# Expert blocks filled by gathers of the tokens' rows, through a table of token numbers by slot, in place of a scatter of those rows

## Chip, cores and metric

One core of one Trainium2 chip runs the whole program. The metric is device time in microseconds (us) of one launch; the median of several runs is given. Everything is fp32.

## The reference, cut to what matters

Two layers over 384 tokens of width 1024: 128 context tokens and 256 latent tokens. Layer 0 mixes by gated linear attention and RWKV-7 scans, layer 1 by latent and differential attention. After the mixer, each layer has a top-2 mixture of 16 experts:

```
scores = sigmoid(t @ w_router); sel = scores + b_router
best group of 4 experts (sum of its two highest sel); top 2 experts in it
gates = scores of the two, divided by their sum
hidden = silu(t @ w_gate[e]) * (t @ w_up[e])      # 1024 -> 512
out    = sum over the two experts of gate * (hidden @ w_down[e])   # 512 -> 1024
```

A layer's experts have 16 x 3 weight matrices of 2 MB, about 100 MB in all, which come from memory once. Each token is computed by its two experts alone.

## The kernel before

**Stages.** Layer 0's mixer, its experts (about 560 to 885 us of the profile), layer 1's mixer, its experts (about 1195 to the end). The order of the work is written out by hand for each engine: every engine has its own program, and waits on semaphores. `when(name)` is the moment at which an engine told an event by name; `steps_of(L, step, i, c)` is a step of expert block c.

**Routing.** TensorE (`router`, `scores`) makes the scores; it also transposes the normalised tokens into rows, which ScalarE copies to `htok` (three tiles of 128 tokens). VectorE (`route`, L2344 on) finds each token's two experts, its place within each expert by products with ones that TensorE makes, ranks the experts by their load, and gives each (token, expert) pair a row. It tells "dst" when the 6 x 128 row numbers `rows_i` are there, and "rows" when the experts' numbers by block are in `xtab`, from which SyncE (SP) reads which expert's weights to load.

**Blocks.** The 16 experts are computed as blocks, c = 0 to 15. Ranks 2 to 7 have room for 96 rows (CAP), the others for 64 (SMALL). Blocks 0, 1 and so on alternate between two buffers. Blocks 0 and 1 (experts 0 and 2) are picked straight from `htok` by products with ones and zeros (`rows_pick`). The rows of the other blocks travel through memory: GpSimd (POOL) issues six indirect DMAs (L639) that scatter the 768 rows of `htok` to a tensor `dispatched`, waits until all have landed (L641), and then reads block by block back (L646, L648, L651), each when the buffer is free, which is when the block two before has been transposed.

**One block on TensorE:** transpose its rows (`rows_T`, or `rows_pick`), gate and up (`gate_up`), transpose the hidden rows (`hidden_T`), down (`down`). The program's order is: pick 0, gate_up 0, pick 1, hidden_T 0, gate_up 1, rows_T 2, down 0, hidden_T 1, gate_up 2, rows_T 3, down 1, and so on in pairs. ScalarE and VectorE copy and combine between those; ScalarE stores the outputs of a block to `expert_out`. At the end POOL gathers each token's two output rows from there (L655), and VectorE adds them with their gates.

**Weights.** SP loads the 48 matrices of a layer, in the order gate, up and down of each block interleaved as they are needed, into six places of 2 MB. The first six go before the router is done. Load 7 (up of block 2) and load 8 (down of block 1) stand behind the wait for "rows", as all later ones. Each load waits for its place: a gate's place is free when the gate product of the block two before is done, and so on. All loads of SP share one queue, and so the weights arrive in order.

**Zeros.** In the early mixer, ScalarE writes zeros over the whole of `dispatched` (8.3 MB) and over the last part of `expert_out` (3.4 MB).

Experts with more tokens than room have extra blocks, behind a test that all engines make (`n_extra`); in the profiled execution there were none.

Of the kernel before, what the change touches and what calls it, by code (L numbers as in the profile page):

```python
# [22 lines left out]
P = 128  # L23
# [36 lines left out]
for _n, _w in [("earlier", 128), ("ones", 128), ("tri16", 256), ("pos", 16), ("rank", 16), ("key", 16), ("extra", 144), ("slots", CAP)]:  # L60
    _M[_n] = (_at, _w)
    _at += _w
# [8 lines left out]
FULL0, SMALL0 = LEAD * SMALL, LEAD * SMALL + FULL * CAP  # L71
XROW = FULL * CAP + (NE - FULL) * SMALL
# [32 lines left out]
def build(nc, io, known):  # L105
# [3 lines left out]
    with ExitStack() as ctx:  # L109
# [56 lines left out]
        Xd = nc.dram_tensor("dispatched", (ROWS, D), F32, kind="Internal").ap()  # L166
        Yd = nc.dram_tensor("expert_out", (ROWS, D), F32, kind="Internal").ap()
        arena_words = 27272
# [130 lines left out]
        htok = take(TILES * D).rearrange("p (t d) -> p t d", t=TILES)  # L299
        hot = take(2 * TILES * CAP).rearrange("p (e t n) -> p e t n", e=2, t=TILES)  # L300
# [104 lines left out]
        def _(sp):  # L405
# [15 lines left out]
            def early(l, m, e, place):  # L421
                weights(l, m, e, place, w_place[place])
# [16 lines left out]
            def experts(l):  # L439
# [24 lines left out]
                sp.wait_ge(*when("rows", l))  # L464
                e3, e4 = expert(slice(3, 4)), expert(slice(4, 5))
# [3 lines left out]
                early(l, 2, LEADERS[1], 1)  # L469
                gate_w(L, l, None, 3, 1, e3)  # L470
# [17 lines left out]
                with sp.If(n_extra > 0):  # L488
# [3 lines left out]
                    with sp.Fori(0, NX) as i:  # L492
# [4 lines left out]
                        sp.wait_ge(*steps_of(X, "xT_p", i, -1))  # L497
                        sp.dma_start(xb[0:CAP, 0, :], Xd[bass.ds(i * CAP + XROW, CAP), :]).then_inc(X["rows"][0][0], 16)
# [27 lines left out]
        def _(pool):  # L526
# [103 lines left out]
            def experts(l):  # L630
# [55 lines left out]
        def _(pe):  # L686
# [852 lines left out]
        def _(act):  # L1539
# [33 lines left out]
            def gate_rows(l, s):  # L1573
                if l == 0 and s == 0:
                    act.wait_ge(sem("xd_zero"), 32)
# [257 lines left out]
            def experts(l):  # L1833
# [5 lines left out]
                silu(L, None, 1, 1, SMALL)  # L1839
                for c in range(LEAD):  # L1840
                    rows_copy(L, None, c + 2, c)
                    store(L, None, c, c, slice(c * SMALL, (c + 1) * SMALL), SMALL)
                    silu(L, None, c + 2, c, cap_of(c + 2))
                with act.Fori(1, half - 2) as i:
                    rows_copy(L, i, 2, 0)
                    store(L, i, 0, 0, bass.ds(i * CAP + (FULL0 - CAP), CAP), CAP)
# [1101 lines left out]
```

## Time and profile before

| | |
|---|---|
| median of 3 runs | 1517.27 us (1516.02 to 1518.22) |
| profiled execution, its own time | 1523.06 us |
| its span, first to last instruction | 1521.3 us |
| mean granted TensorE clock | 0.926 |
| TensorE matmuls busy | 1308.7 us (86%) |
| VectorE, ScalarE, GpSimd busy | 522.0, 337.8, 164.7 us |
| DMA | 355.18 MB, mean 233 GB/s |
| scatters of rows | 12 (6 a layer) |
| expert weight loads | 96 of 2048 KB, 24.5 us in the median from issue to landing |

Each engine's busy time is a mean over stages with different limits, and so it doesn't say what sets the end of one. The rows further down are read by stage: the chain of waits says what released what, the windows give the engines' busy time, the granted clock and the share of the DMA engines in a stretch, and the timelines give single instructions. A DMA's landing time runs from its issue to its last semaphore update. A DMA share of 1.0 means that all 16 engines move data all the time.

### The profile page before, as it was taken

Reading aid. Unit: us, or ns where it says so; the run is one execution under the profiler, and the core shown is the slowest. Engines: PE = TensorE matmul, PEld = TensorE weight load, DVE = VectorE, ACT = ScalarE, POOL = GpSimd, SP = SyncE. Lnnn points to the kernel's source line nnn. Section 1 sums busy time; section 2 is a strip of 40 time slices with the busy share of each in tenths; the row PEclk is TensorE's granted clock in tenths of the full one; section 3 lists DMA queues with packets and bytes.
Section 4 is the critical chain, followed back from the end, with each engine's and each line's share of the span. In section 5 each row is a group of like instructions: output and inputs, shape, how many; then the busy total and the mean of one; then the engine's idle time right before and its main releaser. Section 6 shows DMA issues by size and latency. Waiting matters only on the chain.

```text
span 1521.3 us, 38803 instructions
## 1 busy us (share of the span) xinstructions
PE 1308.7 (86%) x16856; PEld 911.4 (60%) x16856; DVE 522.0 (34%) x1148; ACT 337.8 (22%) x671; POOL 164.7 (11%) x238
## 2 busy tenths in 40 slices
PE   5989999989998987699898669877899859998882
PEld 2448844468887455478776334455574637877651
DVE  1324444145556734011111053457544521111103
ACT  2223221143223131000000043333541300000001
POOL 2003310024333001000000030010000010000001
PEclk8999999999999989799999969988979888999997
DMA  9841159831001175799999882234304478999995
GB/s 396 300 156 59 59 201 315 301 145 59 29 33 59 56 287 214 279 382 379 397 403 417 358 305 76 91 112 181 135 32 166 177 306 304 377 396 395 386 422 194
DMA packets 42230, 355.18 MB, mean 233 GB/s; under 512 B 5707, under 2 KB 10651, under 8 KB 23792
## 3 DMA queue, kind: packets, MB, share of 16 engines
q1 hardware_dynamic: 21456, 302.11, 50.3%
q0 software_dynamic: 8832, 29.07, 5.7%
q10 hardware_dynamic: 11808, 22.03, 4.4%
q8 instruction: 107, 1.75, 0.5%
q14 instruction: 27, 0.22, 0.0%
HBM read 322.17 MB, written 31.01 MB: 232 GB/s over the span
## 4 chain that ended last, share of the span: by engine, by line
PE 65%; DMA 18%; DVE 7%; issue 7%; ACT 3%; POOL 1%; SPq 0%; ACTq 0%; POOLq 0%; DVEq 0%
PE PB L695 59%; DMA arena<-in_w_moe 11%; PE PB L698 6%; DVE arena L2019 3%; DMA dispatched<-arena,rows_i 3%; ACT arena L1546 1%; DMA ring<-in_w_mod 1%; DMA expert_out<-arena 1%; DMA arena<-expert_out,rows_i 1%; DVE small L2032 1%; POOL dispatched L639 1%; DVE arena L2026 1%; DMA arena<-dispatched 1%; DVE x L2019 0%; DVE arena L2023 0%
## 5 line engine op out<-in xcount | busy, mean ns | idle before, releaser
L695 PE MATMUL PB<-arena 64*64 64x64 f32 (+8 forms) x9500 | 478.5, 297 | 45.8 <-DMA arena<-in_w_moe 31.2
L695 PEld LDWEIGHTS PB<-arena 64*64 64x64 f32 (+3 forms) x9500 | 374.4, 131 | 144.9 <-issue 77.1
L695 PE MATMUL PB<-ring,hT 128*128 128x512 f32 (+1 forms) x720 | 314.0, 592 | 7.2 <-DVE hT L2022 3.6
L695 PEld LDWEIGHTS PB<-ring,hT 128*128 128x128 f32 x720 | 137.4, 194 | 167.4 <-issue 162.7
L695 PE MATMUL PB<-ring,arena 128*32 128x256 f32 (+2 forms) x3712 | 209.3, 380 | 9.8 <-DMA ring<-in_w_moe 6.9
L695 PEld LDWEIGHTS PB<-ring,arena 128*32 128x32 f32 x3712 | 171.4, 110 | 39.1 <-issue 9.7
L698 PE MATMUL PB<-cst,arena 128*128 128x128 f32 (+2 forms) x758 | 117.1, 296 | 83.7 <-DMA arena<-dispatched 40.5
L1546 ACT ACTIVATE arena<-PB 128x256 f32<-128x256 f32 (+3 forms) x217 | 106.4, 490 | 330.2 <-PE PB L695 279.1
L698 PEld LDWEIGHTS PB<-cst,arena 128*128 128x128 f32 (+2 forms) x758 | 90.0, 155 | 128.4 <-issue 43.4
L2442 DVE TENSOR_TENSOR arena<-arena,PB 128x256 f32<-128x256 f32 (+1 forms) x32 | 15.1, 471 | 284.6 <-PE PB L695 165.8
L550 POOL TENSOR_TENSOR arena<-arena,cst 128x256 f32<-128x256 f32 x72 | 49.2, 699 | 264.9 <-DVE arena L2019 245.2
L695 PE MATMUL PB<-ring,scT 128*32 128x512 f32 x384 | 57.6, 716 | 22.2 <-DMA ring<-in_w_mod 16.2
L2019 DVE TENSOR_TENSOR arena<-arena,PB 128x256 f32<-128x256 f32 (+1 forms) x116 | 51.0, 440 | 72.0 <-PE PB L695 68.0
L2019 DVE TENSOR_TENSOR arena<-arena 128x512 f32<-128x512 f32 (+7 forms) x120 | 68.1, 567 | 10.5 <-ACT arena L1546 6.4
L1807 ACT ACTIVATE arena<-PB 128x384 f32<-128x384 f32 x32 | 15.7, 491 | 235.7 <-PE PB L698 209.1
L2029 DVE COPY arena<-PB 128x512 f32<-128x512 f32 (+5 forms) x60 | 30.9, 515 | 102.2 <-PE PB L695 94.0
L2453 DVE COPY arena<-PB 128x256 f32<-128x256 f32 (+1 forms) x32 | 15.2, 474 | 131.9 <-PE PB L695 131.9
L1820 ACT ACTIVATE arena<-PB 128x256 f32<-128x256 f32 (+1 forms) x32 | 13.6, 424 | 144.2 <-PE PB L695 144.2
L1813 ACT ACTIVATE arena<-PB 128x256 f32<-128x256 f32 (+1 forms) x32 | 13.5, 423 | 141.4 <-PE PB L695 141.4
L1546 ACT ACT_TABLE_LOAD x27 | 34.6, 1283 | 37.2 <-DVE small L2022 19.6
L1546 ACT ACTIVATE gate<-PB 128x512 f32<-128x512 f32 x40 | 23.9, 597 | 67.8 <-PE PB L695 67.4
L695 PE MATMUL PB<-arena,cst 128*128 128x512 f32 (+1 forms) x80 | 35.8, 642 | 2.7 <-ACT arena L1546 2.7
(150 smaller groups left out, 905.2 us busy)
## 6 DMA issues: line engine op xcount, KB each, us to landing
arena<-in_w_moe SPq DMA_DIRECT2D x50, 2048.0 KB, 24.5
ring<-in_w_moe SPq DMA_DIRECT2D x46, 2048.0 KB, 24.6
ring<-in_w_mod SPq DMA_DIRECT2D x24, 2048.0 KB, 8.3
ring<-in_w_mix SPq DMA_DIRECT2D x22, 2048.0 KB, 8.7
dispatched<-gate ACTq DMA_DIRECT2D x1, 8320.0 KB, 51.4
arena<-dispatched POOLq DMA_DIRECT2D x12, 384.0 KB, 10.9
arena<-dispatched POOLq DMA_DIRECT2D x16, 256.0 KB, 9.3
expert_out<-gate ACTq DMA_DIRECT2D x1, 3456.0 KB, 22.2
```

What stands on the lines that cost most here:

```text
L550: nc.gpsimd.tensor_tensor(out, a, b, ALU.mult).then_inc(*tick("pool", *name))
L639: pool.indirect_dma_start(Xd, bass.IndirectOffsetOnAxis(ap=rows_i[:, 3 * ch + t:3 * ch + t + 1], axis=0), htok[:, t, :], None).then_inc(se ...
L695: return nc.tensor.matmul(out, lhsT, rhs, start=start, stop=stop, **k)
L698: return nc.tensor.transpose(out, in_, ident[0:n, 0:n])
L1546: step(nc.scalar.activation(out, in_, f, **k), *name)
L1807: nc.scalar.activation(xT[:, b, 0:4 * CAP], PB[:, 0, 0:4 * CAP], ACT.Copy).then_inc(L["S"]["xT_a"], 1)
L2019: step(V.tensor_tensor(out, a, b, op), *name)
L2026: step(V.scalar_tensor_tensor(out=out, in0=a, scalar=s, in1=b, op0=op0, op1=op1), *name)
L2029: step(V.tensor_copy(out, a), *name)
L2032: step(V.tensor_reduce(out, a, AX.X, op), *name)
L2442: V.tensor_tensor(hid[:, b, 0:n], sil[:, b, 0:n], PB[:, 4 + b, 0:n], ALU.mult).then_inc(L["S"]["hid"], 1)
L2453: V.tensor_copy(yb[:, b, n:2 * n], PB[:, 7, 0:n]).then_inc(L["S"]["y_v"], 1)
```

## The change

Empty slots and rows are laid out anew. Every block, by rank, has 96 rows in `expert_out`, though it still uses 64 or 96 of them; so a slot's number is 96 times its block's rank plus its place. From the slot of each (token, expert) pair VectorE makes two arrays of ones and zeros: `at_row` (which of 96 places) and `at_block` (which of 25 blocks, times the token's number). Six small products on TensorE (`table`) sum them to a table of 96 by 25 token numbers, which VectorE copies as integers to `tab`; an empty slot has token 0. TensorE makes the table at the head of block 1's pick; VectorE's copy stands behind "rows".

ScalarE stores `htok`, tile by tile, to a tensor `tokens` in memory as soon as each tile is copied (three DMAs of 512 KB). POOL waits for those and for the table, and then issues one indirect DMA a block that gathers its rows (96 or 64) from `tokens` into the block's buffer. The scatters, the wait for them, the tensor `dispatched` and its zeros are gone; in their place zeros go over rows 64 to 95 of each of the 16 blocks in `expert_out` (2 MB). POOL's loop over blocks is written out, and it tests for extra blocks itself; their rows were loaded by SP before.

On SP, the wait for "rows" and the two reads of expert numbers move behind loads 7 and 8, which need no number that is computed.

The diff, with only constants, renamed semaphores and the store's row arithmetic left out:

```diff
+RANK = [0, 1, 2, 8, 3, 9, 4, 10, 5, 11, 6, 12, 7, 13, 14, 15]
+XROW = NE * CAP
...
+        tab = ctx.enter_context(nc.sbuf_tensor("tab", [P, 32], I32))
+        Hd = nc.dram_tensor("tokens", (NTOK, D), F32, kind="Internal").ap()
...
-                sp.wait_ge(*when("rows", l))
-                e3, e4 = expert(slice(3, 4)), expert(slice(4, 5))
                 sp.wait_ge(*steps_of(L, "ga", None, 0))
                 early(l, 1, LEADERS[2], 0)
                 sp.wait_ge(*steps_of(L, "gu", None, 0))
                 early(l, 2, LEADERS[1], 1)
+                sp.wait_ge(*when("rows", l))
+                e3, e4 = expert(slice(3, 4)), expert(slice(4, 5))
...
-                pool.wait_ge(sem("xd_zero"), 32)
-                pool.wait_ge(*when("dst", l))
-                for t in range(TILES):
-                    pool.wait_ge(*when("htok", l, t))
-                    for ch in range(2):
-                        pool.indirect_dma_start(
-                            Xd, bass.IndirectOffsetOnAxis(ap=rows_i[:, 3 * ch + t:3 * ch + t + 1], axis=0),
-                            htok[:, t, :], None).then_inc(sem("dispatched"), 16)
-                pool.wait_ge(sem("dispatched"), 96 * (l + 1))
                 L = base_loop[l]
-                with pool.Fori(1, half - 1) as i:
-                    pool.wait_ge(*steps_of(L, "xT_p", i, -2))
-                    pool.dma_start(xb[0:CAP, 0, :], Xd[bass.ds(i * CAP + (FULL0 - CAP), CAP), :]).then_inc(x_land[0], 16)
-                    pool.wait_ge(*steps_of(L, "xT_p", i, -1))
-                    pool.dma_start(xb[0:SMALL, 1, :], Xd[bass.ds(i * SMALL + (SMALL0 - SMALL), SMALL), :]).then_inc(x_land[1], 16)
-                for b in range(2):
-                    pool.wait_ge(*steps_of(L, "xT_p", None, NE - 4 + b))
-                    pool.dma_start(xb[0:SMALL, b, :], Xd[XROW - (2 - b) * SMALL:XROW - (1 - b) * SMALL, :]).then_inc(x_land[b], 16)
+
+                def gather(b, cap, col, landed):
+
+                    pool.indirect_dma_start(xb[0:cap, b, :], None, Hd,
+                                            bass.IndirectOffsetOnAxis(ap=tab[0:cap, col:col + 1], axis=0)).then_inc(landed, 16)
+
+                pool.wait_ge(sem("h_stored"), 48 * (l + 1))
+                pool.wait_ge(*when("table", l))
+                for c in range(2, NE):
+                    if c >= 4:
+                        pool.wait_ge(*steps_of(L, "xT_p", None, c - 2))
+                    gather(c % 2, cap_of(c), RANK[c], x_land[c % 2])
+                n_extra = nc.gpsimd.value_load(xtab[0:1, 31:32], min_val=0, max_val=NX)
+                with pool.If(n_extra > 0):
+                    X = extra_loop[l]
+                    pool.wait_ge(*steps_of(L, "xT_p", None, NE - 2))
+                    for i in range(NX):
+                        pool.wait_ge(*steps_of(X, "xT_p", None, i - 1))
+                        gather(0, CAP, NE + i, X["rows"][0][0])
...
+            def table(l):
+
+                pe.wait_ge(*when("blocks", l))
+                claim(3, "table", l)
+                for j in range(6):
+                    ins = mm(PB[0:CAP, 3, 0:NE + NX], at_row[:, j, :], at_block[:, j, :], j == 0, j == 5)
+                ins.then_inc(*tick("pe", "table_p", l))
+
             def rows_pick(L, l, c):
 
                 pe.wait_ge(*when("hot", l, c))
+                if c == 1:
+                    table(l)
...
-                        act.dma_start(Xd.rearrange("(b p) d -> p b d", p=80), bc(zeros[0:80, :], 1, ROWS // 80))\
-                            .then_inc(sem("xd_zero"), 16)
+                        act.dma_start(Yd[0:XROW, :].rearrange("(b p) d -> p b d", p=CAP)[SMALL:CAP, :, :], bc(zeros[SMALL:CAP, :], 1, NE))\
+                            .then_inc(sem("y_zero"), 16)
...
+                    act.wait_ge(*when("htok", l, t))
+                    act.dma_start(Hd[t * P:(t + 1) * P, :], htok[:, t, :]).then_inc(sem("h_stored"), 16)
...
-                ts(base, rk, float(LEAD + FULL), float(LEAD), ALU.min, ALU.max)
-                ts(base, base, float(CAP - SMALL), float(LEAD * (CAP - SMALL)), ALU.mult, ALU.subtract)
-                stt(base, rk, float(SMALL), base, ALU.mult, ALU.add)
+                ts(base, rk, float(CAP), None, ALU.mult, None)
...
-                    red(rec[:, 0:3], v16(f))
-                    cp(rows_i[:, 3 * ch:3 * ch + 3], rec[:, 0:3], *(("dst", l) if ch else ()))
+                    red(picked[:, 3 * ch:3 * ch + 3], v16(f))
+
+                nb = NE + NX
+                ge6 = c2[:, 0:6 * (nb + 1)].rearrange("p (j b) -> p j b", j=6)
+                tt(ge6, bc(picked, 2, nb + 1), bc(M("edge"), 1, 6), ALU.is_ge)
+                red(block, ge6[:, :, 1:nb + 1])
+                tt(at_block, ge6[:, :, 0:nb], ge6[:, :, 1:nb + 1], ALU.subtract)
+                tt(at_block, at_block, bc(M("token"), 2, nb), ALU.mult)
+                stt(place_in, block, -float(CAP), picked, ALU.mult, ALU.add)
+                tt(at_row, bc(place_in, 2, CAP), bc(M("low"), 1, 6), ALU.is_equal, "blocks", l)
+                cp(rows_i[:, :], picked, "dst", l)
...
+                dve.wait_ge(*when("table_p", l))
+                cp(tab[0:CAP, 0:nb], PB[0:CAP, 3, 0:nb], "table", l)
```

## Rows read from the trace of the kernel before

**Rows 1.** Chain of waits, layer 0's entry: start us, us, what
```profile
593.19 24.34 DMA dispatched<-arena,rows_i
618.42 4.13 DMA arena<-dispatched
```

**Rows 2.** Windows: us, engines' busy us (instructions), PEclk, DMA share, GB/s
```profile
570.00:585.00 15.00, 13.32 (x146) 11.17 (x150) 11.94 (x49) 4.27 (x8) 0.00 (x0) 1.00 0.01 2
610.00:620.00 10.00, 0.00 (x0) 0.00 (x0) 0.00 (x0) 0.00 (x0) 1.12 (x2) 0.50 0.69 286
620.00:632.00 12.00, 9.40 (x110) 6.01 (x114) 1.31 (x3) 0.88 (x2) 0.53 (x1) 0.66 0.42 107
632.00:712.00 80.00, 80.00 (x1382) 63.89 (x1375) 10.39 (x21) 7.21 (x16) 2.57 (x5) 1.00 1.01 386
712.00:855.00 143.00, 123.91 (x2018) 95.88 (x2020) 16.33 (x35) 11.20 (x25) 3.08 (x6) 0.96 1.01 405
```

**Rows 3.** Timeline of SP's queue, both layers: start us, us, line, operation, tiles, count
```profile
590.66 0.33 SPq L419 DMA_DIRECT2D ring<-in_w_moe  x1
...
598.53 0.34 SPq L419 DMA_DIRECT2D ring<-in_w_moe  x1
...
629.81 0.34 SPq L419 DMA_DIRECT2D arena<-in_w_moe  x1
...
1234.50 0.34 SPq L419 DMA_DIRECT2D ring<-in_w_moe  x1
1237.80 27.21 SPq L419 DMA_DIRECT2D arena<-in_w_moe  x2
```

**Rows 4.** Timeline of VectorE, end of the routing of layer 0
```profile
585.72 0.17 DVE L2029 CAST rows_i<-arena 128x3 int32<-128x3 f32 x1
585.92 0.31 DVE L2019 TENSOR_TENSOR arena<-arena 128x144 f32<-128x144 f32 x1
...
588.58 0.17 DVE L2029 CAST xtab<-arena 128x16 int32<-128x16 f32 x1
```

**Rows 5.** Timeline of TensorE, layer 0; in brackets idle us before it, and releaser
```profile
570.36 2.18 PE L695 MATMUL PB<-small,arena 128*128 128x16 f32 x18 [0.54 <-DVE small L2019]
...
588.05 5.43 PEld L695 LDWEIGHTS PB<-arena 128*128 128x128 f32 x48 [0.41 <-DVE arena L2019]
...
598.13 3.64 PE L695 MATMUL PB<-arena 128*32 128x256 f32 x64
...
622.60 1.54 PE L698 MATMUL PB<-cst,arena 96*128 96x96 f32 x8 [20.82 <-DMA arena<-dispatched]
```

**Rows 6.** Timeline of POOL: a scatter of layer 0, a gather at its end
```profile
586.76 1.04 POOL L639 DMA_INDIRECT dispatched<-arena,rows_i  x1 [32.02 <-DVE arena L2032]
...
874.21 0.94 POOL L655 DMA_INDIRECT arena<-expert_out,rows_i  x1 [0.30 <-issue]
```

**Rows 7.** DMA issues of 871:885, 712:855, 499:500, 629.5:630, 1264.5:1265: KB each, us to landing
```profile
arena<-expert_out,rows_i POOLq DMA_INDIRECT x6, 5.7
...
arena<-dispatched POOLq DMA_DIRECT2D x2, 384.0 KB, 11.0
...
ring<-in_w_moe SPq DMA_DIRECT2D x1, 2048.0 KB, 7.7
...
arena<-in_w_moe SPq DMA_DIRECT2D x1, 2048.0 KB, 8.9
...
arena<-in_w_moe SPq DMA_DIRECT2D x1, 2048.0 KB, 9.4
```

**Rows 8.** DMA queues of 712:855, then 871:885: packets, MB, share of engines
```profile
q0 software_dynamic: 544, 1.84, 4.0%
...
q0 software_dynamic: 864, 3.15, 63.5%
```

**Rows 9.** The zero fill's issue, and the chain of waits beside it
```profile
dispatched<-gate ACTq DMA_DIRECT2D x1, 8320.0 KB, 51.4
...
233.60 70.22 PE PB L695 x196
```

More of the change, by code:

```diff
@@ L59 @@
 CAP = SETS * GRP
-for _n, _w in [("earlier", 128), ("ones", 128), ("tri16", 256), ("pos", 16), ("rank", 16), ("key", 16), ("extra", 144), ("slots", CAP)]:
+for _n, _w in [("earlier", 128), ("ones", 128), ("tri16", 256), ("pos", 16), ("rank", 16), ("key", 16), ("extra", 144), ("slots", CAP),
+               ("edge", NE + 10), ("low", CAP), ("token", 6)]:
     _M[_n] = (_at, _w)
@@ L299, in build @@
         htok = take(TILES * D).rearrange("p (t d) -> p t d", t=TILES)
+        at_row = take(6 * CAP).rearrange("p (j n) -> p j n", j=6)
+        at_block = take(6 * (NE + NX)).rearrange("p (j n) -> p j n", j=6)
         hot = take(2 * TILES * CAP).rearrange("p (e t n) -> p e t n", e=2, t=TILES)
@@ L1574, in gate_rows @@
                 if l == 0 and s == 0:
-                    act.wait_ge(sem("xd_zero"), 32)
+                    act.wait_ge(sem("y_zero"), 32)
                 for n in range(4):
@@ L1839, in experts, with rows_of @@
                 silu(L, None, 1, 1, SMALL)
+                def rows_of(c):
+                    return slice(CAP * RANK[c], CAP * RANK[c] + cap_of(c))
                 for c in range(LEAD):
                     rows_copy(L, None, c + 2, c)
-                    store(L, None, c, c, slice(c * SMALL, (c + 1) * SMALL), SMALL)
+                    store(L, None, c, c, rows_of(c), SMALL)
                     silu(L, None, c + 2, c, cap_of(c + 2))
@@ L1845, in experts @@
                     rows_copy(L, i, 2, 0)
-                    store(L, i, 0, 0, bass.ds(i * CAP + (FULL0 - CAP), CAP), CAP)
+                    store(L, i, 0, 0, bass.ds(i * CAP + CAP, CAP), CAP)
                     silu(L, i, 2, 0, CAP)
                     rows_copy(L, i, 3, 1)
-                    store(L, i, 1, 1, bass.ds(i * SMALL + (SMALL0 - SMALL), SMALL), SMALL)
+                    store(L, i, 1, 1, bass.ds(i * CAP + 7 * CAP, SMALL), SMALL)
                     silu(L, i, 3, 1, SMALL)
-                rows_copy(L, None, NE - 2, 0)
-                store(L, None, NE - 4, 0, slice(SMALL0 - CAP, SMALL0), CAP)
-                silu(L, None, NE - 2, 0, SMALL)
-                rows_copy(L, None, NE - 1, 1)
-                store(L, None, NE - 3, 1, slice(XROW - 3 * SMALL, XROW - 2 * SMALL), SMALL)
-                silu(L, None, NE - 1, 1, SMALL)
-                for b in range(2):
-                    store(L, None, NE - 2 + b, b, slice(XROW - (2 - b) * SMALL, XROW - (1 - b) * SMALL), SMALL)
+                for c in (NE - 2, NE - 1):
+                    rows_copy(L, None, c, c % 2)
+                    store(L, None, c - 2, c % 2, rows_of(c - 2), cap_of(c - 2))
+                    silu(L, None, c, c % 2, SMALL)
+                for c in (NE - 2, NE - 1):
+                    store(L, None, c, c % 2, rows_of(c), SMALL)
                 n_extra = nc.scalar.value_load(xtab[0:1, 31:32], min_val=0, max_val=NX)
@@ L2338, in route @@
                 cum, xbk, off, ov, rec = w(16), w(16), w(16), w(16), w(4)
+                block, place_in = w(6), w(6)
                 key, rk, base, cap = w(16), w(16), w(16), w(16)
@@ L2851, in constants @@
     for name, v in (("earlier", a < b), ("ones", 1.0), ("pos", np.arange(NE)), ("extra", np.arange(16 * NX) // 16),
-                    ("rank", [0, 1, 2, 8, 3, 9, 4, 10, 5, 11, 6, 12, 7, 13, 14, 15]),
+                    ("rank", RANK), ("edge", CAP * np.arange(NE + NX + 1)), ("low", np.arange(CAP)),
+                    ("token", np.tile(P * np.arange(TILES)[None, :] + a, (1, 2))),
                     ("key", (NE - 1 - np.arange(NE)) / 32 + 1000 * np.array([3, 1, 2] + [0] * (NE - 3))),
```

9 lines of the change are left out of this document (2 added, 7 removed).

## The prediction

> **What bounds the kernel now.** I read the chain of waits first. On entering the experts of layer 0 it leaves TensorE for a DMA: from the last scatter's issue at 593.19 it waits 24.34 us for the scattered rows, then 4.13 us for block 2's rows to be read back [rows 1]. TensorE goes on at 622.60, after 20.82 us of idleness [rows 5]. The windows say what that costs. From 610 to 620 TensorE does nothing, and from 620 to 632 the DMA engines too are only 0.42 busy, at 107 GB/s: the stream of expert weights has run dry. From 632 to 855 the DMA share is 1.01, at 386 and 405 GB/s, while TensorE, never idle before 712, waits 19 of the 143 us after it [rows 2]. So the end of the stage is the moment at which the stream restarts plus a fixed amount of bytes, and the stall costs what it delays the restart. The SP queue shows how: it issues a 2 MB load when its place is free. Of the 48 loads of a layer, numbers 7 and 8 come late, from 590.66 on, number 9 at 598.53, and number 11 (the down weights of block 2) only at 629.81, because block 0's down product stands behind the wait for block 2's rows. Layer 1 repeats it: load 9 at 1234.50, then two issues that span 27.21 us from 1237.80, so load 11 at 1264.7 [rows 3].
>
> **The first stretch, step by step (layer 0).**
> DVE. Gone: two operations on the block bases and two casts, 0.2 us each with the gap (one cast starts at 585.72, the next work at 585.92). The slots, without the second cast, are there 0.6 us before 585.7, at 585.1. New before "blocks": a compare of 156 elements, a reduce, two operations of 150 (0.31 us each, as the one of 144), a small one (0.2), and a compare of 576: between 0.31 and four times that, 0.8 taken. With gaps 2.4 us, so "blocks" at 587.5. Then the cast and the same 2.8 us of work to "rows", told at 588.75 today: now 590.6, and the table's copy out of PSUM 590.8 [rows 4].
> TensorE comes to the table behind block 0's gate and up, where block 1's pick starts today at 588.05, 0.5 us after "blocks": no wait. Six products of 25 columns at 0.12 us, as 18 of 16 columns took 2.18, and the start: 0.9 us. Everything behind moves by it: block 1's up, which ends at 601.8 today, ends at 602.7; block 2's transposes could start by 603.6 at the latest, counting 0.9 for semaphores [rows 5].
> ACT issues three stores of the tokens' rows ahead of the gate copies. I cost them at nothing: the 1.5 MB move while the DMA engines are idle (share 0.01 from 570 to 585 [rows 2]), and TensorE's use of the gate copies has other work ahead. Without that cover the three issues, each at most POOL's 1.04 us, would cost up to 3 us a layer.
> SP. The wait for "rows" moves behind loads 7 and 8. They then go when their places are free, the up's end at 588.05 and 3.6 us ahead of it, so at about 584.7 and 588.4, and land by 598. Load 9 needs "rows" and two register reads (1.9 us, from 588.75 to 590.66 today): 592.5, before its place is free at 599.4, 0.9 later than today.
> POOL's first scatter starts 0.9 us after the slots are told; so the gather for block 2 starts at 591.7, that for block 3 1.3 us later [rows 6]. Six scatters, the wait for them and the read-back are gone.
> How soon a gather lands beside weight loads is not in the trace. Bounds: 5.7 us, as the six gathers at the end, and 24.3, as the last of the six scatters. I take 11.0, which a direct 384 KB block load takes in the full stream [rows 7]: the same bytes in the same company, and 160 rows are a fifth of the scatters' 768. Block 2's rows land at 602.7; TensorE wants them at 603.6. No stall. Block 3's are wanted behind block 0's down, past 608.
>
> **The restart.** The transposes took 1.54 us at the low clock (the granted clock is 0.50 and 0.66 there [rows 2]), 0.8 at the full one; block 0's down took 5.7 and takes 3.6, as the 64 products of block 1 [rows 5]. So load 11 is issued at 608.1, before load 10 has landed, and the stream restarts with load 9, at 599.4. In a quiet queue 2 MB land 7.7 us after issue, and in the stream each takes 2.1 MB / 405 GB/s = 5.2 us. Load 9 lands at 607.2, loads 10 and 11 10.4 us later. Block 4's rows and block 0's store, which today come on idle engines, add 0.39 + 0.26 MB, 1.7 us. Load 11 lands at 619.3; today at 629.81 + 8.9 = 638.7 [rows 3, 7]. Gain 19.4 us. The next loads follow block 2's gate and up, 1.5 times 3.64 us each, against 5.2 of transfer: they are asked for just in time, and the stream holds. Behind it stand the same 37 loads.
> Layer 1: load 9 at 1235.4, landed 1243.1, load 11 at 1255.2; today 1264.7 + 9.4 = 1274.1. Gain 18.9, less 0.3 because its gather, by the same steps, starts at 1227.8 and lands at 1238.8 against a TensorE that arrives at 1238.7: 18.6.
> What is late next is the weight stream, as after 712 today.
>
> **Steady state.** Block loads become gathers of the same bytes, 1 us of an idle POOL each. Their share of the DMA engines: over 712 to 855 the 544 packets of the software queue took 4.0% of 16 engines, 168 ns each; the gathers of 871 to 885, 864 packets at 63.5% of 14 us, 165 ns each [rows 8]. Equal, so 0; the bounds are in rival B. POOL's register read and branch stand behind the last gather, with two blocks still to compute. The zero fill shrinks from 8.3 to 2 MB; the old one took 51.4 us to land, beside 70.22 us of TensorE without a wait [rows 9]: 0. Should the new fill be slow, it is wanted only behind the output projection.
>
> **Sum.** 19.4 + 18.6 = 38.0 us. The profiled execution took 1523.06 us (span 1521.3 and 1.8 around it): it would take 1485.1. It lay 5.8 over the median of the runs, 1517.27; from that, 1479.3.
> By the fit of 2.0 us plus bytes / 436 GB/s in the Trainium skill (DMA: Bandwidth & Descriptors, Anatomy of one DMA) a gather of 393 KB would land in 2.9 us, an estimate. The trace's direct load of that size needs 11.0 in the full stream, so the measurement decides; by either there is no stall and the sum is the same.
>
> **Rivals.**
> A, the first gathers land late. For it: the last scatter's 24.3 us, and that loads 7 and 8 are in flight. Against it: a fifth of the rows. At that bound: 591.7 + 24.3 = 616.0, the down done at the low clock by 623.2, load 11 landed at 632.1, gain 6.6; in layer 1 5.4. Time 1505.
> A2, DVE keeps POOL from making descriptors. Bound: both gathers held for DVE's longest stretch beside POOL here, 2.8 us each. Block 2's rows at 608.3, the down at 612.7, load 11 landed 2.3 us later than forecast, in layer 1 3: 1485. Against it: the first scatter, issued beside busy DVE, took 1.04 us, a later gather with DVE idle 0.94 [rows 6]. The Trainium skill (SBUF — State Buffer, SBUF: two separate sides) states this lock for DMAs issued from GpSimd; here it cost at most 0.1 us.
> B, gathered rows cost the stream more. 1216 slots hold 768 rows, so 448 are empty and point at token 0: one row of memory is read again and again, and no row here shows that. In the stream the gathers are 928 packets a layer, 9.7 us at 168 ns, 19.5 in both. At twice that the gain is 18.5: 1499.
> C, slower than before: the same mechanism past the point where it eats 38 us, 2.9 times or 490 ns a packet. At 3.5 times it takes 49: 1528. Against it, the equal price of gathered and direct rows.
> D, no change: the table comes so late that TensorE waits as before. DVE would need 19 us more; I count 2.
>
> **Chances.** Forecast 0.80 (1473 to 1487); A and A2 0.12; B 0.04; C 0.03; D 0.01. The range for 8 in 10 takes in A2 and the near part of A and B: 1472 to 1493. By over 0.2%, what can be told from no change: faster 0.96, within 0.01, slower 0.03.
>
> **What would show it.** No scatter; TensorE's idleness ahead of block 2's transposes under 2 us; load 11 issued at 608; no window below 0.9 of DMA share from 602 to the stage's end; the granted clock at 1.0 there; packets of the software queue at 165 to 170 ns. I am wrong if the two gathers land past 604 and 1239 by more than 2 us, if the stream has a hole behind load 9, or if its rate falls below 400 GB/s.

## The result

After the change the median is 1484.33 us (1483.24 to 1489.46, four runs), before it 1517.74 us (1516.02 to 1519.74, four runs beside them): a ratio of 0.9766, 95% interval 0.9739 to 0.9793, or 33.4 us less. A second comparison gave 0.9768 (0.9725 to 0.981). The forecast was 1479.3 us and 38.0 us. The profiled execution took 1489.46 us (span 1487.5) against 1523.06: 33.6 us less.

To see where they went I cut every profile into four by loads of SP: the mixer of layer 0 (start to the first two ring loads of its experts' weights, "the mark"), its experts (to the first load of layer 1's mixer weights), the mixer of layer 1 (to its own mark), and its experts (to the last store of the output).

| us | mixer 0 | experts 0 | mixer 1 | experts 1 |
|---|---|---|---|---|
| before | 552.0 | 332.2 | 303.1 | 331.0 |
| after | 553.2 | 312.0 | 307.8 | 311.4 |
| difference | +1.2 | -20.2 | +4.7 | -19.6 |

The two expert stages gained 39.8 us (forecast 38.0). The two mixers, which the change hardly touches, lost 5.9. A single pair of profiles gives this to within 2 or 3 us only: three profiles with the expert stages of before (two more are below) have 332.2, 331.0 and 329.0 us in layer 0 and 331.0, 329.6 and 330.4 in layer 1. Three with those of after have 312.0 each, and 311.4, 310.2 and 311.2. By the means the gain is 18.7 and 19.4, together 38.1 us.

### The profile page after: what moved, and what is told of

Its sections match the earlier page's. It is cut to its first block, busy times and chain, and to the rows that moved or that the text cites. A ratio compares the mean times of both kernels' runs of the same rounds, so it can differ in the third digit from the quotient of the medians.

```text
span 1487.5 us, 38763 instructions
## 1 busy us (share of the span) xinstructions
PE 1311.6 (88%) x16880; PEld 915.6 (62%) x16880; DVE 525.2 (35%) x1156; ACT 337.8 (23%) x671; POOL 163.6 (11%) x226
## 2 busy tenths in 40 slices
DMA packets 39799, 345.75 MB, mean 232 GB/s; under 512 B 5611, under 2 KB 10555, under 8 KB 21360
## 4 chain that ended last, share of the span: by engine, by line
PE 65%; DMA 18%; issue 7%; DVE 6%; ACT 3%; ACTq 0%; DVEq 0%; POOLq 0%; POOL 0%; SPq 0%
PE PB L699 60%; DMA arena<-in_w_moe 15%; PE PB L702 6%; DVE arena L2037 3%; DMA ring<-in_w_mod 2%; ACT arena L1560 1%; DVE small L2050 1%; DMA expert_out<-arena 1%; DVE x L2037 1%; DVE arena L2044 0%; ACT hT L1560 0%; DMA arena<-expert_out,rows_i 0%; ACT L1560 0%; DVE arena L2047 0%; ACT ring L1560 0%
## 5 line engine op out<-in xcount | busy, mean ns | idle before, releaser
L699 PE MATMUL PB<-arena 64*64 64x64 f32 (+7 forms) x9524 | 477.1, 294 | 50.7 <-DMA arena<-in_w_moe 37.2
L699 PE MATMUL PB<-ring,scT 128*32 128x512 f32 x384 | 60.8, 753 | 21.9 <-DMA ring<-in_w_mod 16.0
L2037 DVE TENSOR_TENSOR arena<-arena 128x512 f32<-128x512 f32 (+7 forms) x128 | 71.5, 558 | 10.8 <-ACT arena L1560 6.4
L640 POOL DMA_INDIRECT arena<-tokens,tab x28 | 25.5, 911 | 432.7 <-PE PB L702 357.7
L2047 DVE COPY arena<-PB 128x512 f32<-128x512 f32 (+5 forms) x60 | 30.9, 515 | 102.9 <-PE PB L699 87.2
L1821 ACT ACTIVATE arena<-PB 128x384 f32<-128x384 f32 x32 | 15.7, 491 | 201.1 <-PE PB L702 172.4
L699 PEld LDWEIGHTS PB<-ring,scT 128*32 128x32 f32 x384 | 11.2, 127 | 45.0 <-issue 34.8
```

Of the source, the lines that this page charges most:

```text
L640: pool.indirect_dma_start(xb[0:cap, b, :], None, Hd, bass.IndirectOffsetOnAxis(ap=tab[0:cap, col:col + 1], axis=0)).then_inc(landed, 16)
L699: return nc.tensor.matmul(out, lhsT, rhs, start=start, stop=stop, **k)
L1821: nc.scalar.activation(xT[:, b, 0:4 * CAP], PB[:, 0, 0:4 * CAP], ACT.Copy).then_inc(L["S"]["xT_a"], 1)
L2037: step(V.tensor_tensor(out, a, b, op), *name)
L2047: step(V.tensor_copy(out, a), *name)
```

## The profile after

The whole run reaches layer 0's experts 1.2 us later than before, so times of layer 0 are to be read less 1.2. VectorE at the end of the routing (start us, us, operation), for [rows 4]:

```profile
587.93 0.76 DVE L2037 TENSOR_TENSOR arena<-arena 128x576 f32<-128x576 f32 x1
588.72 0.17 DVE L2047 CAST rows_i<-arena 128x6 int32<-128x6 f32 x1
...
591.58 0.17 DVE L2047 CAST xtab<-arena 128x16 int32<-128x16 f32 x1
591.79 0.18 DVE L2047 CAST tab<-PB 96x25 int32<-96x25 f32 x1
```

The compare of 576 elements took 0.76 us (0.8 was taken). "blocks" comes at 588.69, "rows" at 591.75 and the table at 591.97: less 1.2, the forecast's 587.5, 590.6 and 590.8. POOL's first gathers, for [rows 6]:

```profile
592.85 0.98 POOL L640 DMA_INDIRECT arena<-tokens,tab  x1 [36.91 <-DVE tab L2047]
594.13 0.91 POOL L640 DMA_INDIRECT arena<-tokens,tab  x1 [0.30 <-issue]
```

and their landings, then that of load 9, each from the DMA issues of a stretch that holds it alone, for [rows 7]:

```profile
arena<-tokens,tab POOLq DMA_INDIRECT x1, 9.3
...
arena<-tokens,tab POOLq DMA_INDIRECT x1, 8.4
...
ring<-in_w_moe SPq DMA_DIRECT2D x1, 2048.0 KB, 9.0
```

Block 2's rows are there at 602.1 (11.0 us from the issue were taken, 9.3 came), and TensorE, for [rows 5], does not stop for them:

```profile
600.42 3.64 PE L699 MATMUL PB<-arena 128*32 128x256 f32 x64
603.99 0.88 PE L702 MATMUL PB<-cst,arena 96*128 96x96 f32 x8
604.80 3.66 PE L699 MATMUL PB<-arena 128*32 128x256 f32 x64
```

The brackets with the idle time are gone, where 20.82 us stood. The transposes took 0.88 us at the full clock against 1.54, block 0's down 3.66. SP's queue, for [rows 3]:

```profile
585.99 0.33 SPq L423 DMA_DIRECT2D ring<-in_w_moe  x1
589.44 0.33 SPq L423 DMA_DIRECT2D arena<-in_w_moe  x1
600.82 0.34 SPq L423 DMA_DIRECT2D ring<-in_w_moe  x1
604.12 4.74 SPq L423 DMA_DIRECT2D arena<-in_w_moe  x2
```

Loads 7, 8 and 9 at 584.8, 588.2 and 599.6 on the old time base (forecast 584.7, 588.4, 599.4); the pair of the last row ends in load 11 at 608.5, 607.3 on the old base (608.1). Some of load 11's completion records are missing, so its landing can't be given. Load 8 landed at 600.8 and load 9 at 609.8, on the old base 599.6 and 608.6, which is 1.6 and 1.4 us later than forecast.

Layer 1 does the same, 14.2 us earlier than before: its first gather starts at 1213.23 and lands 10.2 us later, at 1223.4, and TensorE begins block 2's transposes at 1224.42 without a wait. On the old base these are 1227.4, 1237.6 and 1238.6, where the forecast had 1227.8, 1238.8 and 1238.7.

The windows, for [rows 2] (us, busy us by engine, granted clock, DMA share, GB/s):

```profile
586.00:601.00 15.00, 14.33 (x202) 11.30 (x198) 6.75 (x22) 1.19 (x3) 1.89 (x2) 1.00 0.91 324
601.00:604.00 3.00, 3.00 (x61) 1.57 (x49) 0.00 (x0) 0.06 (x1) 0.00 (x0) 1.00 0.78 216
604.00:612.00 8.00, 8.00 (x138) 6.11 (x138) 1.74 (x4) 0.87 (x2) 0.91 (x1) 1.00 1.02 397
612.00:694.00 82.00, 79.10 (x1344) 62.43 (x1339) 10.00 (x20) 7.21 (x16) 4.54 (x5) 0.98 1.01 390
694.00:836.00 142.00, 123.21 (x2028) 95.92 (x2018) 16.73 (x35) 11.20 (x25) 5.43 (x6) 0.98 1.01 406
```

Of the hole of [rows 2] 3 us at a share of 0.78 are left, between load 8's landing at 600.8 and the data of load 9, which was issued at that moment. The rate behind it is first 390 and then 406 GB/s, as it was before (386, 405); the forecast's 5.2 us a load took 405 from the start (2.1 MB at 390 are 5.4). The gathers in the steady state, for [rows 8]:

```profile
q0 software_dynamic: 544, 1.84, 4.0%
```

the same count and share as before, over 142 us (167 ns a packet). The zero fill over `expert_out`'s blocks, for [rows 9], and the chain of waits beside it:

```profile
expert_out<-gate ACTq DMA_DIRECT2D x1, 2048.0 KB, 12.5
```

```profile
232.95 70.22 PE PB L699 x196
```

12.5 us instead of 51.4, and TensorE's chain is as long as it was. Over the whole run the DMA engines moved 345.75 MB instead of 355.18; TensorE was busy for 1311.6 us (1308.7 before), at a mean granted clock of 0.934 (0.926).

## What all profiles have in common

This reading came out of the experiments, and it explains them all, so it stands ahead of them. Take the first 100 us behind the mark, and the rest of the stage. Before:

```profile
552.00:652.00 100.00, 71.75 (x904) 55.45 (x907) 28.34 (x95) 16.68 (x31) 8.65 (x11) 0.83 0.65 252
652.00:884.20 232.20, 199.51 (x3175) 152.40 (x3166) 29.46 (x59) 21.76 (x45) 10.89 (x16) 0.95 0.98 387
```

After:

```profile
553.20:653.20 100.00, 93.11 (x1299) 75.53 (x1299) 33.13 (x105) 18.64 (x35) 6.16 (x7) 0.93 0.82 309
653.20:865.20 212.00, 174.88 (x2788) 131.42 (x2788) 26.53 (x53) 19.75 (x41) 12.89 (x14) 0.95 0.98 390
```

The rest is moved at 386 to 391 GB/s in all ten profiles that I cut so. So a stage of layer 0 takes 100 us, and then the bytes that are left at that rate. That bytes and rate give the length is true by definition; what the profiles show is that the rate and the bytes in all hardly change, so that the length follows from the bytes of the first 100 us. Before: 115.1 MB in all, less 25.2, at 387 GB/s: 232.3 us. After: 113.6 - 30.9 = 82.7 MB at 390: 212.0. The 20.2 us are then 5.7 MB more in the first 100 us (14.7 us), 1.5 MB less in all (3.9), and the rate (1.6).

## Experiments

None of these kernels beats the one after but the short load, which leaves work out. Each set was compared with runs of the kernel before on the same chip (medians 1520.81, 1521.22 and 1520.03 us). A diff is against the kernel after, or against the one before where the heading says so. The last column has the lengths of the two expert stages in the profiled execution.

| kernel | median us | ratio (95%) | experts 0, 1 |
|---|---|---|---|
| before, again | (1520.91, one run) | | 331.0, 329.6 |
| after, again | 1484.39 | 0.9768 (0.9725-0.981) | 312.0, 310.2 |
| after, SP waits for rows first | 1498.65 | 0.9849 (0.9812-0.9886) | 318.7, 316.6 |
| after, one row | 1708.28 | 1.1231 | 312.6, (535.2) |
| after, empty slots spread | 1485.13 | 0.9769 | 312.0, 311.5 |
| after, gathers later | 1499.27 | 0.9865 (0.9845-0.9885) | 320.6, 318.5 |
| after, gathers latest | 1510.17 | 0.9922 (0.9897-0.9947) | 326.2, 323.3 |
| before, block 0's down first | 1526.34 | 1.004 (1.0014-1.0065) | 332.1, 331.6 |
| before, loads 7, 8 first | 1511.62 | 0.9943 (0.9915-0.997) | 326.3, 325.0 |
| after, a short load | 1478.21 | 0.9727 (0.9705-0.9749) | 309.5, 306.1 |
| before, mixer shifted | (1526.19, one run) | | 329.0, 330.4 |
| after, mixer shifted | (1486.97, one run) | | 312.0, 311.2 |

**The kernel after, once more.** No edit.

> The changed kernel once more, with nothing edited, to see whether the 4.7 us that layer 1's mixer took more in its profile (from SP's first mixer load at 865.27 to its first expert load into the ring at 1173.09, 307.8 us; 303.1 in the kernel before) come again. Theory (chance of the granted clock): the mixer's length follows how much of it falls in spells of the low clock, and so it will differ from 307.8 by some us either way in this profile; the timed ratio stays at 0.977 to 0.979. Rival (the change itself lengthens the mixer, by its table, its DMAs or its memory layout): 307 to 308.5 again.

Measured 1484.39 us; both stages are there again within 1.2 us. Its mixers took 548.9 and 305.2 us, 4.3 and 2.6 less than in the first profile, outside the rival's 307 to 308.5: what the mixers lost changes from run to run.

**SP's order undone.**

```diff
+                sp.wait_ge(*when("rows", l))
+                e3, e4 = expert(slice(3, 4)), expert(slice(4, 5))
                 sp.wait_ge(*steps_of(L, "ga", None, 0))
                 early(l, 1, LEADERS[2], 0)
                 sp.wait_ge(*steps_of(L, "gu", None, 0))
                 early(l, 2, LEADERS[1], 1)
-                sp.wait_ge(*when("rows", l))
-                e3, e4 = expert(slice(3, 4)), expert(slice(4, 5))
```

> The changed kernel with one part undone: SP waits for the experts' numbers again before loads 7 and 8. They then go at about 593.7 and 594.1 and not at 586.0 and 589.4, together with the two gathers. Theory (the stream of weights sets the end): load 9, issued at 600.8 as before, finds load 8 still under way and lands about 2.7 us later in each layer: 1484.3 + 5.4 = 1489.7, and if the gathers are late beside two loads, up to 1493. Rival (TensorE sets the end, and it needs load 7 only at 609): 1484.3, no change.

Measured 14.3 us more than after, more than either bound. The first 100 us and the rest:

```profile
550.40:650.40 100.00, 92.06 (x1277) 75.34 (x1280) 33.18 (x105) 18.64 (x35) 6.16 (x7) 0.93 0.75 281
650.40:869.10 218.70, 178.84 (x2812) 133.72 (x2804) 26.55 (x53) 19.55 (x41) 12.90 (x14) 0.94 0.98 390
```

TensorE works nearly as much (92.06 against 93.11 us), but 2.8 MB less are moved: at 390 GB/s 7.2 us, and the stage is 6.7 longer. From 30 to 40 us after the mark next to nothing is moved (2 GB/s), and loads 7 and 8 are then in flight beside the gathers and ahead of load 9, which landed 12.2, 15.7 and 18.0 us after their issues (9.3, 8.4 and 9.0 in the kernel after). TensorE waits only 1.05 us for the rows and is 1.4 us late when load 12 is asked for. It pays later: its first wait for weights comes 105.6 us after the mark, in the kernel after 133.5 us after it.

**Rows read again and again (rival B).** First all slots read token 0, so that all blocks but the first two compute with that token alone; then only the empty slots are changed, and each of a block reads another token.

```diff
-                cp(tab[0:CAP, 0:nb], PB[0:CAP, 3, 0:nb], "table", l)
+                ts(tab[0:CAP, 0:nb], PB[0:CAP, 3, 0:nb], 0.0, None, ALU.mult, None, "table", l)
```

> The changed kernel with the table multiplied by zero, so that every slot of every gathered block reads token 0 (the output is then another; the bytes, packets and instructions are the same). In the changed kernel some 320 of 1088 gathered rows of a layer already read that row. Theory (where a row lies does not matter): software-queue packets stay at 165 to 170 ns in the full stream, time 1484 within 2 us. Rival (reads of one row again and again are slow): the packets get 2 to 3 times longer, the stream loses 10 to 20 us a layer, 1504 to 1525.

```diff
-                cp(tab[0:CAP, 0:nb], PB[0:CAP, 3, 0:nb], "table", l)
+                ts(c2[0:CAP, 0:nb], PB[0:CAP, 3, 0:nb], 0.5, M("spread")[0:CAP, :], ALU.is_lt, ALU.mult)
+                stt(tab[0:CAP, 0:nb], PB[0:CAP, 3, 0:nb], -1.0, c2[0:CAP, 0:nb], ALU.add, ALU.add, "table", l)
```

(the table holds token + 1, and `spread` a token number by place)

> The changed kernel with empty slots pointing at different tokens (1 plus 3 times the place, less one) instead of all at token 0, for one more small VectorE operation in front of the gathers (0.2 us). Theory (where a row lies does not matter): 1484.5 to 1485, within noise of the changed kernel. Rival (the empty slots' common row slows the gathers): faster by what that costs, 1478 to 1483.

With one row the stage of layer 0 took 312.6 us against 312.0, and in its full stream the 544 packets of the software queue took 3.8% of the engines (159 ns each) against 4.0% (167 ns). Layer 1 can't be read: the wrong rows changed its routing, and it had nine extra blocks with 27 more weight loads, and there lie all of the 224 us by which this kernel is longer. Spread, the median is 1485.13 us, as after. Rival B is out: reading one row of memory many times costs nothing here that can be seen.

**Later gathers.** POOL waits for block 1's gate product (first variant) or its up product (second) before its first gather.

```diff
                 pool.wait_ge(*when("table", l))
+                pool.wait_ge(*steps_of(L, "ga", None, 1))    # second variant: "gu"
```

The second variant was run first:

> The kernel after, but POOL also waits for the end of block 1's up product before its first gather. Held against the kernel after (1484.3 us). My theory: a stall of TensorE costs only what it delays the restart of the weight stream. The gathers go at 605 instead of 592, land 9 us later (614), TensorE stands still for about 10 us, block 0's down ends at 620 instead of 608.5, load 11 is asked for then, by when load 10 (604) has landed; so the stream has a hole of some 6 us, 6 to 7 us a layer: 1497 us (1494 to 1500). Rival 1, TensorE's stall counts one for one: 11 us a layer, 1506. Rival 2, the bytes alone set the end, the stall is made up in the later stream: 1484.

> The kernel after, but POOL's first gathers wait for the end of block 1's gate product (its up product in e5_late_gather), so they start at 601 instead of 593. It gives the slope between 'no stall' (1484 us) and e5 (13.55 us of idle TensorE in layer 0, TensorE 15.7 us late, 13 us a layer, 1510). Theory after e5: TensorE also paces the loads 12, 13 and so on; what it is late is given on, less a slack of some 2.5 us. Rows landed by 613 (12 us), TensorE idle for 8 us, 10 us late with the low clock behind it, 7.5 us a layer: 1499 us (1496 to 1502). Rival, my prediction's picture (only the moment at which load 11 is asked for counts, and it may be late by the time that load 10 needs): 3 us a layer or less, 1490.

TensorE's timeline, second variant and then first:

```profile
618.37 1.54 PE L703 MATMUL PB<-cst,arena 96*128 96x96 f32 x8 [13.55 <-DMA arena<-tokens,tab]
```

```profile
608.29 1.54 PE L703 MATMUL PB<-cst,arena 96*128 96x96 f32 x8 [9.27 <-DMA arena<-tokens,tab]
```

Measured 1510.17 us, against 1497, 1506 and 1484: all three missed, and rival 1 by least. Gathers beside load 9 land after 12.6 us and not 9, and the idle TensorE falls to the low clock (1.54 us for the transposes, 4.56 for the down). By its next load after the hole, load 12, it is 16.8 us late, and the stage 14.2 us longer. The first variant, with the theory made from this, came out at 1499.27 us against 1499 forecast (load 12 is 11.1 us late, the stage 8.6 longer); the picture that only load 11 counts gave 1490. Its two windows, for the bytes:

```profile
548.20:648.20 100.00, 83.84 (x1110) 67.17 (x1113) 32.05 (x103) 17.66 (x33) 5.25 (x6) 0.88 0.76 282
648.20:868.80 220.60, 189.48 (x2981) 140.27 (x2972) 27.54 (x55) 20.35 (x42) 13.79 (x15) 0.94 0.98 387
```

2.7 MB less, 6.9 us, and 1.7 by the rate: 8.6, as measured.

**Block 0's down ahead of block 2's rows, in the kernel before.**

```diff
                     for n in (1, 2):
                         c = at + n
-                        rows_T(L, i, c + 1, (n + 1) % 2)
-                        down(L, i, c - 1, (n - 1) % 2, caps[n - 1])
+                        if i is None and at == 0 and n == 1:
+                            down(L, i, c - 1, (n - 1) % 2, caps[n - 1])
+                            rows_T(L, i, c + 1, (n + 1) % 2)
+                        else:
+                            ...      # the two lines in their old order
```

> The kernel BEFORE (scatter and read-back kept), with block 0's down product ahead of the transposes of block 2's rows in the first pair, both layers. It takes the order on TensorE alone: load 11's place is free at about 606 instead of 629.8, though TensorE waits for the rows as long. My theory (the restart of the stream and the bytes behind it set the end): load 11 moves in the hole, TensorE goes on at 622.6 with the transposes and block 2's gate, load 12 is asked for at 628 instead of 635.7; 6 to 8 us a layer, so 1504 us against 1518 (1502 to 1508). Rival, only the earlier rows count (TensorE's stall is the cost, one for one): 4 to 6 us a layer at most for the down product that fills the stall, and nothing for the stream: 1508 or later; if the end hangs on the rows' landing alone, 1518.

Slower by 0.4% in the median of twelve runs; the profiled execution, with 1521.12 us one of the fastest, has its expert stages as before, so where the other 5 us went is not shown. SP's queue shows that the edit did what it should (the second row of two ends in load 11, at 606.4), and then nothing until load 12:

```profile
599.66 0.34 SPq L419 DMA_DIRECT2D ring<-in_w_moe  x1
602.96 3.79 SPq L419 DMA_DIRECT2D arena<-in_w_moe  x2
633.50 0.33 SPq L419 DMA_DIRECT2D ring<-in_w_moe  x1
```

Load 12 is asked for 83.9 us after the mark, before it was 83.6. Its place comes free with block 2's gate, behind the rows; and the rows came later. The chain of waits:

```profile
590.77 22.82 DMA dispatched<-arena,rows_i
...
614.48 9.32 DMA arena<-dispatched
```

The read-back takes 9.32 us, where it took 4.13 on idle DMA engines [rows 1]: it now runs beside loads 10 and 11. So the rows land 3.7 us later from the mark than before, and block 2's gate and up, now the first long work behind the hole, take 11.91 us against 10.69. Together with two short waits that eats the 5.67 us of the earlier down. The bytes in the first 100 us are 25.0 MB, before 25.2.

**Loads 7 and 8 ahead of "rows", in the kernel before.** SP's part of the change alone; the diff is the inverse of the one above.

> The kernel BEFORE with loads 7 and 8 ahead of SP's wait for rows, as in the change; scatter and read-back kept. My theory: 0 to 2 us (1516 to 1520): loads 7 and 8 go some 3 to 6 us earlier, but load 9's place is free only at 598.5, load 11 still waits for block 0's down behind the scattered rows, and the hole ahead of it stays; the two loads collide a bit more with the scatter. Rival: the order is worth by itself the 14 us that it was worth in the kernel after (1504). Rival 2: the scatter, now beside two loads in flight from its first packet on, lands later, and the kernel gets slower: 1522 to 1528.

9.6 us faster (4.6 to 12.9 by the interval), which neither the theory (0 to 2) nor its rivals (14 faster, or slower) had. The chain of waits says why:

```profile
589.53 16.47 DMA dispatched<-arena,rows_i
...
606.89 8.19 DMA arena<-dispatched
```

The last scatter lands 16.47 us after its issue against 24.34 [rows 1]. The DMA queues (packets, MB, share) of 592 to 604 before, with loads 7 and 8 in flight:

```profile
q1 hardware_dynamic: 253, 3.88, 76.6%
q0 software_dynamic: 256, 0.92, 22.9%
```

and of 588 to 597 in this kernel:

```profile
q1 hardware_dynamic: 161, 2.11, 55.1%
q0 software_dynamic: 377, 1.41, 38.2%
```

Before, weights (q1) and scattered rows (q0) take packets one for one, 21 rows' packets a us; a weight packet (15 KB in the mean) takes 76.6% of 16 times 12 us over 253, that is 0.58 us, a row's (3.6 KB) 0.17. With the loads gone ahead, the scatter gets 42 a us. That is a mean over two conditions: from 588 to 592 there are 209 of its packets against 58 of weights (52 a us), from 592 to 596 84 against 87, and so 21 a us again. The Trainium skill (DMA: Bandwidth & Descriptors, Queues, rings and completion order) says that each DMA engine goes round-robin between its queues, packet by packet; 256 against 253 and 84 against 87 packets agree. So a transfer of small packets is slowed by a large load in flight beside it, by much more than its share of the bytes; that is what the wait for "rows" had cost here, and the late gathers of the SP experiment fit it.

**The kernel before, once more.**

> The kernel before, unchanged, for a second profile. The profile of the change showed 5.9 us lost in the two mixers (1.2 and 4.7), which its edits hardly touch. If the clock's chance did that, this profile's mixers lie between 547 and 553 us (layer 0) and 303 and 308 (layer 1), as those of the kernels after did; if the change costs layer 1's mixer something, it is at 303 again. The two expert stages: 332 and 331 us.

Measured 1520.91 us, with mixers of 552.5 and 303.1 us and expert stages of 331.0 and 329.6. By the words of the expectation the 303.1 spoke for a cost of the change in layer 1's mixer, and not for chance; the last two experiments were made for that.

**A short load.**

```diff
-                gate_w(L, l, None, 4, 0, e4)
+                sp.wait_ge(*steps_of(L, "ga", None, 2))
+                sp.dma_start(...[:, 0:CHUNK // 8], ...[:, 0:CHUNK // 8])
```

> The kernel after, but load 12 of each layer (the gate weights of block 4) moves only an eighth of its 2 MB; the outputs of one expert are not the reference's (and routing in layer 1 may change a little). If bytes left at the full stream set the stage's end, 1.84 MB less at 390 GB/s are 4.7 us a layer: 1475 us (1473 to 1477). Rival, TensorE's own work sets the end from where it restarts: 1484, no change.

6.2 us faster than after, where 9.4 and 0 stood: nearer to the bytes. The rest of the stage:

```profile
647.70:857.20 209.50, 177.19 (x2788) 133.49 (x2788) 26.56 (x53) 20.03 (x41) 12.86 (x14) 0.94 0.98 386
```

1.8 MB less to move, but at 386 and not 390 GB/s, which gives 2.1 of the 4.7 us back in layer 0: the stream does not run at the same rate all the time, and neither the bytes alone nor TensorE alone sets the end. In the kernel after, TensorE first waits for weights at 686.8 us (2.90 us), 133.5 us after the mark; until then its own products set when loads are asked for.

**Why the mixers lost time.** Three profiles with the expert stage of before have 303.1, 303.1 and 303.2 us for the mixer of layer 1; the nine whose stage of layer 0 is shorter have 303.4 to 309.1, 307.0 in the mean, and the one with only SP's order changed is among them (307.3), so it isn't the gathers. TensorE's work there is the same. The granted clock differs, as over 100 us of attention, 100 us after the mixer's first load; before (second profile) and after:

```profile
983.50:1083.50 100.00, 75.47 (x421) 49.22 (x422) 60.41 (x123) 38.33 (x75) 7.56 (x15) 0.86 0.38 135
```

```profile
965.30:1065.30 100.00, 79.61 (x393) 50.76 (x391) 58.56 (x116) 36.63 (x71) 7.54 (x15) 0.80 0.36 134
```

0.86 against 0.80, a mean over spells at 1.2 and at 2.4 GHz. The test shifts the work by VectorE operations that do nothing, at the head of the mixer, in the kernel before and in the one after:

```diff
                 y0, y1 = yg[:, t, :], yg[:, 3 + t, :]
+                if (l, t) == (0, 0):
+                    for _ in range(4):
+                        ts(y0, y0, 1.0, None, ALU.mult, None)
```

> The kernel BEFORE with four more VectorE multiplications by 1.0 (0.75 us each, some 3.1 us in all) at the junction from the experts of layer 0 to the mixer of layer 1; nothing else. Three profiles with the old stage 0 showed that mixer at 303.1, 303.1 and 303.2 us (from the first load of its weights to the first load of layer 1's experts), six with another stage 0 at 305.2 to 309.1, with the same work in it. Theory: the spells of the low granted clock fall at times of their own, on other work as soon as the work is shifted: then this one is not 303.1 + 3.1 = 306.2 but off by 1 us or more (307 to 312). Rival: the spells belong to the work, and the loss has another cause (gathered rows, TensorE denser in stage 0): 306.2 +- 0.3.

> The kernel AFTER with the same four multiplications. By the theory of e11 the mixer of layer 1 lies anywhere in 303 to 309 plus 3.1; by its rival, at 307.8 + 3.1 = 310.9, as the six profiles of this kind had a mean of 307.8, less their scatter of 1.4. It alone decides little; with e11 it tells whether the shift moves the spells.

Each was run once, for its profile. The kernel before with the shift:

```profile
979.70:1079.70 100.00, 79.56 (x380) 50.06 (x378) 56.81 (x108) 34.50 (x65) 7.54 (x15) 0.80 0.36 133
```

Its mixer took 311.3 us: 3.0 by the edit (VectorE's first work in the mixer starts that much later behind the first load) and some 5 more, with a clock that is 0.80 now here too. Its stage of layer 0 also came out 2 us shorter than the least of the three, without an edit there, so more than the 3 us had moved. The kernel after with the shift took 308.4, so 305.4 without it, where the rival had 307.8. So the clock over the mixer changed when the work was shifted by a few us, and the old kernel lost as much by it as the change did; this rests on one profile of each. The Trainium skill (TensorE: Matmul & The Clock Gate, Part 1: The HAM clock gate (the "warmup" mystery)) says that the gate's timing does not start with the kernel, so that the same kernel varies. The two profiles of the kernel after (307.8 and 305.2) fit that; the three with the old stage, which agree within 0.1 us, do not, and why is open.

## Why the prediction was right, and where it was not

- **The first stretch** holds step by step: the table, the gathers' starts and loads 7, 8, 9 and 11 were issued within 0.8 us of the forecast, and TensorE's stall of 20.82 us is gone. Rivals A, A2 and D needed late rows; the rows were 1.9 us ahead of TensorE in layer 0 and 1.0 in layer 1.
- **The sum**: 19.4 us in layer 0, 20.2 measured in this pair of profiles and 18.7 by the means; 18.6 in layer 1, 19.6 and 19.4 measured. It is right within what profiles of one kernel differ by (3.2 us in layer 0 before).
- **"The stall costs what it delays the restart"** is right only with another restart than the one I named. I took load 11 as the mark. With load 11 asked for 21 us earlier the kernel before gained nothing; what counts is when TensorE goes on past the rows, since loads 12, 13 and so on wait for its products. A TensorE 16.8 us late cost 14.2 us in layer 0, one 11.1 us late 8.6. In the change itself both move alike (loads 11 and 12 both go 22.5 us earlier from the mark), so the sum could not tell them apart, and that it holds with load 11 as the mark is luck. TensorE's restart alone is not the whole either: with SP's order undone it is 1.4 us late and the stage 6.7 longer. The bytes moved in the first 100 us go with the stage's length in all the runs. The price of rival A was about right, for it kept TensorE waiting: rows at 616.0 were to cost 12.8 us in layer 0 (a gain of 6.6 and not 19.4), and the latest gathers landed them at 617.9 on this base and cost 14.2.
- **SP's move** I priced as two earlier loads and as no gain of its own. Alone it is worth 9.6 us of the 36 that stand between 1521 and 1484, by letting the scatter through; in the kernel after it is worth 14.3. The gathers without it are worth 22.2. The parts do not overlap: 9.6 and 22.2 are 31.8, somewhat less than the 36.4 of both. Whether they help each other is not settled; by the expert stages alone, in means, the parts are 9.7 and 25.7 us, together 35.4 of 38.1.
- **Bytes**: the 1.5 MB less in the stage (six scatters of 512 KB out, three stores in) I had left out. They make 3.9 us of the 20.2 in the count by bytes. They are no further gain on top of the forecast's sum, which compares the landings of load 11 with the same loads behind it: scatters and stores are over by then.
- **Signs of being wrong**: two of those named came. The stream's rate was to be 400 GB/s or more and was 390 from 612 to 694 us; the row of before that was read for the forecast had 386 in the same place, and 405 only later. And a window of 3 us had a DMA share of 0.78, where none was to be below 0.9. Both are worth little in time, 0.2 us a load and under 1 us.
- **The low clock** in the stall's wake was in the sum (1.54 and 5.67 us against 0.88 and 3.66); the granted clock behind it came to 0.98, not 1.0.
- **Mixers**: I took them as unchanged. That is the term that failed: they lost 5.9 us in the profile, more than the 4.6 us by which the measured gain fell short of the forecast. In layer 0 it is chance: over all profiles the mixer took 548.3 to 552.5 us with the old zero fill (550.6 in the mean of five) and 547.6 to 553.2 with the new one (549.6 of nine), so the smaller fill is worth nothing that shows, as forecast. In layer 1 it goes with the granted clock (303.1 us at 0.86, 303.4 to 305.8 at 0.83, 307.3 to 309.1 at 0.80), and the shift by 3 us makes it likely, on one profile, that a change in the work's timing is enough for that.

## What to carry to other kernels

In a stage that a stream of loads ends, integrate: count the bytes that have moved by the time at which the stream is full, and divide what is left by its rate; a single late load says little. When a late transfer goes away, look for what else shares the DMA engines with it: small packets beside large ones got every second turn here. And in a kernel with spells of low clock, a gain of some microseconds in one stage may come back smaller because the later ones are shifted; compare stage by stage before looking for a cause.

## What was not expected of the hardware

- Packets of scattered rows (3.6 KB in the mean) beside weight packets (15 KB): one for one, so 21 a us, against 52 where few weights were in flight.
- A gather of 96 rows from memory landed in 9.3 us behind one load in flight and in 12.2 to 12.6 in other company. Reading one row for every slot showed no cost (159 against 167 ns a packet).
- With VectorE's work shifted by 3.0 us, a mixer of 303 us had a granted clock of 0.80 and not 0.86 over 100 us of it, and took some 5 us more than the shift (one profile).
